# The keys' decay in a gated linear recurrence: a second, backward product scan in place of Ln and Exp

## The reference

```python
f = lb + (1.0 - lb) * sigmoid(f_logit)
k = 1.0 - f
q = silu(q_in) * HG_DK ** -0.5
S_t = diag(f_t) S_{t-1} + k_t^T v_t
o_t = S_t^T q_t
o = rms_norm(o) * silu(o_gate)
```

## Time and profile before

| | us |
|---|---|
| median of 3 runs (2399.16 to 2399.67) | 2399.17 |
| the profiled execution | 2399.41 |
| its span, slowest core (core 7) | 2397.9 |
| spans of all cores | 2392.3 to 2397.9 |

### The profile page before, as it was taken

The page is one execution under the profiler, slowest core; times in us unless marked ns, Lnnn a source line. Parts: engine busy times, 40 slices in busy tenths (PEclk is TensorE's granted clock), DMA queues, the critical chain, the costliest instruction groups (busy, mean ns, idle before and its releaser), DMA issues.

```text
span 2397.9 us, 40703 instructions; the slowest of 8 cores (2392.3 to 2397.9 us)
## 1 busy us (share of the span) xinstructions
PE 2323.3 (97%) x14144; PEld 1168.1 (49%) x14144; DVE 1311.1 (55%) x1977; ACT 1173.2 (49%) x1680; POOL 386.1 (16%) x515
## 2 busy tenths in 40 slices
PE   7999999999999889999999999999999999999998
PEld 3555555556555444444444444444444444444443
DVE  3666665666666874555553544536354545355334
ACT  4787788788888883444442331313222232224120
POOL 4444344344343340000000000000000000000000
PEclk9999999999999999999999999999999999999999
DMA  9566373564560555433335443434344333424240
GB/s 161 90 112 98 64 126 51 100 106 66 101 113 22 143 97 129 106 88 89 90 76 157 123 139 105 159 115 145 128 132 139 125 124 116 139 88 161 79 156 36
DMA packets 95977, 263.59 MB, mean 110 GB/s; under 512 B 9920, under 2 KB 34624, under 8 KB 92224
## 3 DMA queue, kind: packets, MB, share of 16 engines
q1 hardware_dynamic: 77008, 195.69, 25.1%
q0 software_dynamic: 18768, 65.28, 19.0%
HBM read 275.88 MB, written 61.87 MB: 141 GB/s over the span
## 4 chain that ended last, share of the span: by engine, by line
PE 87%; ACT 4%; DVE 4%; issue 3%; POOL 1%; DMA 1%; DVEq 0%; ACTq 0%; POOLq 0%; SPq 0%
PE psb L413 86%; ACT L434 1%; PE psb L418 1%; ACT sb_F L434 1%; DVE sb_YT L482 1%; DVE sb_Tb L466 1%; DVE sb_F L616 1%; DMA sb_W<-w 1%; ACT sb_U L434 0%; ACT sb_rso L434 0%; POOL sb_F L455 0%; DVE sb_ub L466 0%; DMA sb_y<-yD 0%; DVE sb_vt L473 0%; DVE sb_Qp L442 0%
## 5 line engine op out<-in xcount | busy, mean ns | idle before, releaser
L413 PE MATMUL psb<-sb_xT,sb_W 128*128 128x512 bf16 x2560 | 738.2, 383 | 28.2 <-DMA sb_xT<-xt 11.3
L413 PE MATMUL psb<-sb_hT,sb_f1r 128*128 128x512 bf16 x2816 | 681.2, 379 | 0.0
L434 ACT ACT_TABLE_LOAD x271 | 347.7, 1283 | 287.5 <-DVE sb_mv L908 129.7
L413 PEld LDWEIGHTS psb<-sb_hT,sb_f1r 128*128 128x128 bf16 x2816 | 273.4, 98 | 325.9
L413 PE MATMUL psb<-sb_W,sb_xT 128*128 128x128 bf16 x2048 | 402.6, 220 | 5.5 <-DVE sb_vt L473 4.1
L413 PE MATMUL psb<-sb_wf,sb_actb 128*128 128x512 bf16 x1408 | 346.4, 379 | 0.4 <-DVE sb_actb L442 0.3
L413 PEld LDWEIGHTS psb<-sb_xT,sb_W 128*128 128x128 bf16 x2560 | 239.7, 98 | 195.6 <-issue 45.0
L413 PE MATMUL psb<-sb_xT,sb_wj 128*128 128x512 bf16 x1024 | 314.9, 379 | 2.8 <-ACT sb_hT L434 1.3
L442 DVE TENSOR_TENSOR sb_actb<-sb_sg,psb 128x512 bf16<-128x512 f32 x176 | 118.6, 685 | 270.4 <-PE psb L413 168.0
L434 ACT ACTIVATE sb_sg<-psb 128x512 f32<-128x512 f32 x176 | 102.7, 596 | 296.2 <-PE psb L413 294.0
L413 PEld LDWEIGHTS psb<-sb_W,sb_xT 128*128 128x128 bf16 x2048 | 194.5, 98 | 69.4 <-issue 13.5
(11 more groups left out here) (91 smaller groups left out, 2760.3 us busy)
## 6 DMA issues: line engine op xcount, KB each, us to landing
...
```

Source lines behind the costliest of these rows:

```text
L413: return P.add("pe", lambda e: e.matmul(o, lhsT=l, rhs=r, start=start, stop=stop), ks(lhsT, rhs), out.k, dur=max(60, fsz(r)) / 2400.0 + 0. ...
L434: return P.add("act", lambda e: e.activation(out=o, in_=i, func=func, **kw), rd, out.k, dur=0.19 + fsz(o) / 1200.0 + 0.09 * ptr, tbl=ACT_S ...
```

## The change

The keys are no longer divided by D. A second scan, backwards along the frames, gives E, the product of the f from the frame after the key to the end of its half chunk. It reads f shifted by one (the new tile `fg` has one column more than the 512, which holds 1) and resets at the same mask. F3 x E is the key as it enters the state at the half chunk's end. This product is made on POOL now, straight into Kb. The first half's copy in the middle is scaled by e2 instead of e1, so Kb's last two pieces are what Kc was, and Kc and its product are gone; PE transposes Kb itself.

For the scores the query then has to be Qp divided by its half chunk's whole decay: a DVE reciprocal of the 8 end values of a tile into `Ei`, and a POOL product of Qp with it into `Qd`. The forward scan now writes over `fg`. Ln and Exp of D on ACT are gone. Counts per step: ACT loses 2 operations; DVE loses one product (Kb) and gets one scan and one reciprocal; POOL loses one product (Kc) and gets two (Kb, Qd).

```diff
--- before.py
+++ after.py
@@ -345,11 +345,13 @@
         Y2 = b("Y2", [32, 128], F32)
         YT = [b(f"YT{i}", [1024], F32) for i in range(4)]
         conv_end = b.at
-        F = [[b(f"F{i}_{p}", [TS], F32) for i in range(4)] for p in range(2)]
+        F = [[b(f"F{i}_{p}", [TS], F32) for i in range(3)] for p in range(2)]
+        fg = [b(f"fg{p}", [TS + 1], F32) for p in range(2)]
         Qp = [b(f"Qp{p}", [4, 128], BF16) for p in range(2)]
         Qx = [b(f"Qx{p}", [4, 64], BF16) for p in range(2)]
         Kb = [b(f"Kb{p}", [4, 192], BF16) for p in range(2)]
-        K2 = [b(f"Kc{p}", [4, 128], BF16) for p in range(2)]
+        Qd = [b(f"Qd{p}", [4, 128], BF16) for p in range(2)]
+        Ei = [b(f"Ei{p}", [8], F32) for p in range(2)]
         og = [b(f"og{p}", [TS], BF16) for p in range(2)]
         vt = [b(f"vt{p}", [4, 128], BF16) for p in range(2)]
         Kt = [b(f"Kt{p}", [4, 128], BF16) for p in range(2)]
@@ -555,6 +557,9 @@
         memset(scm.all(), 0.0)
         memset(V(scm.h[:, 0:TS:64], scm.all().k), 1.0)
         scanmask = scm.all()
+        endmask = scm.all()
+        for p in range(2):
+            memset(fg[p][TS:TS + 1], 1.0)
 
         one = sgl[0]
         memset(one[0:128], 1.0 / 128.0)
@@ -598,7 +603,7 @@
             if t == 0 and ("h", h) not in Wh:
                 Wh[("h", h)] = [wload(h, q) for q in range(4)]
             wq, wf, wo, wi = Wh[("h", h)]
-            F0, F1, F2, F3 = F[p]
+            F0, F1, F3 = F[p]
             for (w, dst, fn) in ((wf, F1, AF.Tanh), (wq, F0, AF.Silu), (wo, og[p], AF.Silu)):
                 ps = newps()
                 for kc in range(8):
@@ -609,13 +614,31 @@
                 relps(ps)
                 yield
                 if fn == AF.Tanh:
-                    ts(F2.all(), F1.all(), lbt[1, h:h + 1], lbt[3, h:h + 1], ALU.mult, ALU.add, eng="pool")
+                    f = fg[p]
+                    ts(f[0:TS], F1.all(), lbt[1, h:h + 1], lbt[3, h:h + 1], ALU.mult, ALU.add, eng="pool")
                     ts(F3.all(), F1.all(), lbt[2, h:h + 1], lbt[1, h:h + 1], ALU.mult, ALU.add, eng="pool")
 
-                    o, m, i2 = F1.all().ap, scanmask.ap, F2.all().ap
-                    P.add("dve", lambda e, o=o, m=m, i2=i2: e.tensor_tensor_scan(
-                        out=o, data0=m, data1=i2, initial=1.0, op0=ALU.max, op1=ALU.mult),
-                        ks(scanmask, F2.all()), F1.all().k, dur=1.3)
+
+                    fv = f.all()
+                    o, i1, m = F1.h[:, ::-1], f.h[:, TS:0:-1], endmask.ap
+                    P.add("dve", lambda e, o=o, m=m, i1=i1: e.tensor_tensor_scan(
+                        out=o, data0=i1, data1=m, initial=1.0, op0=ALU.mult, op1=ALU.max),
+                        ks(endmask, fv), F1.all().k, dur=1.3)
+                    o, m = f[0:TS].ap, scanmask.ap
+                    P.add("dve", lambda e, o=o, m=m: e.tensor_tensor_scan(
+                        out=o, data0=m, data1=o, initial=1.0, op0=ALU.max, op1=ALU.mult),
+                        ks(scanmask, f[0:TS]), f[0:TS].k, dur=1.3)
+                    kv = Kb[p]
+                    kout = V(kv.h[:].rearrange("p b (s q) -> p b s q", s=3)[:, :, 0:3:2, :], kv.all().k)
+                    tt(kout, V(F3.h[:].rearrange("p (b s q) -> p b s q", b=4, s=2), F3.all().k),
+                       V(F1.h[:].rearrange("p (b s q) -> p b s q", b=4, s=2), F1.all().k), ALU.mult, eng="pool")
+                    f2v = V(f.h[:, 0:TS].rearrange("p (b q) -> p b q", b=4), f[0:TS].k)
+                    e1 = V(f2v.ap[:, :, 63], f2v.k)
+                    e2 = V(f2v.ap[:, :, 127], f2v.k)
+                    tt(kv[:, 64:128], kv[:, 0:64], e2.bc(2, [128, 4, 64]), ALU.mult, eng="pool")
+                    o, i = Ei[p].all().ap, f.h[:, 63:TS:64]
+                    P.add("dve", lambda e, o=o, i=i: e.reciprocal(o, i), f2v.k, Ei[p].all().k, dur=0.25)
+                    tt(Eb[p].all(), e1, e2, ALU.mult, eng="pool")
             ps = newps()
             for tl in range(4):
                 for kc in range(8):
@@ -625,23 +648,12 @@
                     yield
             cp(vt[p].all(), pv3(ps, 4))
             relps(ps)
-            act(F2.all(), F1.all(), AF.Ln)
-            yield
-            f2v = V(F1.h[:].rearrange("p (b q) -> p b q", b=4), F1.all().k)
-            e1 = V(f2v.ap[:, :, 63], F1.all().k)
-            e2 = V(f2v.ap[:, :, 127], F1.all().k)
+            yield
+            q64 = Qp[p].all().r("p b (s q) -> p (b s) q", s=2)
             tt(Qp[p].all(), V(F0.h[:].rearrange("p (b q) -> p b q", b=4), F0.all().k), f2v, ALU.mult)
-            tt(Eb[p].all(), e1, e2, ALU.mult, eng="pool")
+            tt(Qd[p].all().r("p b (s q) -> p (b s) q", s=2), q64, Ei[p].all().bc(2, [128, 8, 64]), ALU.mult, eng="pool")
+            yield
             tt(Qx[p].all(), Qp[p][:, 64:128], e1.bc(2, [128, 4, 64]), ALU.mult)
-            act(F2.all(), F2.all(), AF.Exp, scale=-1.0)
-            yield
-            kv = Kb[p]
-            kout = V(kv.h[:].rearrange("p b (s q) -> p b s q", s=3)[:, :, 0:3:2, :], kv.all().k)
-            tt(kout, V(F3.h[:].rearrange("p (b s q) -> p b s q", b=4, s=2), F3.all().k),
-               V(F2.h[:].rearrange("p (b s q) -> p b s q", b=4, s=2), F2.all().k), ALU.mult)
-            yield
-            tt(kv[:, 64:128], kv[:, 0:64], e1.bc(2, [128, 4, 64]), ALU.mult, eng="pool")
-            tt(K2[p].all(), kv[:, 64:192], e2.bc(2, [128, 4, 128]), ALU.mult, eng="pool")
             yield
 
         def back(s):
@@ -650,7 +662,7 @@
             ps = newps()
             psv = V(psb[ps][:].bitcast(BF16), [("ps", ps)])
             for bb in range(4):
-                tr(V(psv.ap[:, bb * 128:bb * 128 + 128], psv.k), K2[p][bb, :])
+                tr(V(psv.ap[:, bb * 128:bb * 128 + 128], psv.k), Kb[p][bb, 64:192])
             cp(Kt[p].all(), V(psv.ap[:, 0:512].rearrange("p (a b) -> p a b", a=4), psv.k), eng="act")
             relps(ps)
             yield
@@ -658,7 +670,7 @@
             for bb in range(4):
                 for hf in range(2):
                     c0 = bb * 128 + hf * 64
-                    mm(pv(psA, c0, c0 + 64), Kb[p][bb, hf * 64:hf * 64 + 128], Qp[p][bb, hf * 64:hf * 64 + 64], True, True)
+                    mm(pv(psA, c0, c0 + 64), Kb[p][bb, hf * 64:hf * 64 + 128], Qd[p][bb, hf * 64:hf * 64 + 64], True, True)
             tt(Am[p].all(), pv3(psA, 4), mask.bc(1, [128, 4, 128]), ALU.mult)
             relps(psA)
             yield
```

## The result

The changed kernel took 2419.31 us (median of 6 runs, 2418.21 the lowest) against 2399.42 for the kernel before (6 runs): ratio 1.0079, 95% interval 1.0065 to 1.0093, so 19 us slower.

The account below looks back on a forecast made before the run. PE was taken to bound the kernel, 97% busy, with only its 42.5 us stage idle time and 28 us unseen waits recoverable. Terms -6, -5 (-9 and +4), -4 and +1 made -14 from 2399.4: 2385 us, range 2366 to 2405.

Parts of the forecast that it names:

- What goes: ACT loses each tile's Ln and Exp, 80 us, and 42 table loads, 54 us: 134 us in all.
- -6, -9 and -4: Gains in the stage, in us: PE's waits that ACT ends, waits DVE ends because it idles for ACT, unseen waits.
- The new instructions by themselves: Step pricing the added work: DVE 46 us more for second scan and reciprocal less a product, POOL 86 us more.
- The path: From forget gate's Tanh: keys 7.3 us now, 3.9 us to the transposes afterwards; scores 5.1 us; shorter if POOL and DVE are free.
- sum of -14: Total of all terms in us, including +1 for POOL's extra product in front of PE, giving 2385 us.
- The price of blocking: Rival, chance 0.05: DVE and POOL SBUF products block each other, 0.62 us in one tile of three, 13 us: 2398 us.
- My own test: Sign of a wrong forecast: POOL products whose mean is 0.3 us above 1.34.
- DVE's extra time: Term in the stage: DVE's extra 46 us take back a sixth of its idle time, +4 us.
- slower: Rival, chance 0.15: back-to-back scans on DVE delay sb_Am and state updates PE waits for, +28 less 14: 2413 us.
- The waits for ACT: PE's stage waits that ACT ends: 7.2 of 27.7 us, so 11 of the 42.5; half taken, -6 us.
- Tests that didn't fire: Signs of a wrong forecast: PE's waits for sb_Tb, sb_Am, sb_vt above 25 us together, or for sb_Qd above 5.
- Outside the stage: Sign: nothing changes from 1400 us on; a gain outside the stage would show the forecast wrong.

Follow-up runs that it names:

- e1: Kernel before without Ln and Exp of the forget product, keys multiplied by the decay instead of divided (computation changed): 2385.5 us, ratio 0.9943.
- e5: Control for e4: changed kernel with seven PSUM banks in the first stage, scans' mask in SBUF as before: 2453.5 us, ratio 1.0220.
- e4: Changed kernel with the scans' mask read from a PSUM bank, leaving seven banks for the first stage's matmuls: 2410.6 us (one run), no ratio.
- e10: Kernel before with a second scan into a scratch tile, result unused, both scans' mask in PSUM, seven banks: 2430.6 us, ratio 1.0124.
- e15: e11 with the key value F3 made on ACT instead of POOL and the key product on DVE: 2405.5 us, ratio 1.0015.
- e13: e11 with the key value F3 made on ACT in place of POOL: 2401.9 us, ratio 1.0000.
- e11: Changed kernel with the two scans in the other order, forward first, then backward: 2406.5 us, ratio 1.0022.

## Why the prediction was wrong

Forecast 2385 (2366 to 2405), measured 2419. The balance over the 40 tiles from the 8th to the 48th, where before to after is +17.8 us:

- ACT's relief, e1 less before: 530.9 - 541.0 = **-10**.
- The meetings, e5 less e4, on one and the same order: **+21**.
- The second scan in DVE's queue, e10 less before, less the bank: 553.8 - 541.0 - 6.3 = **+7**; if the bank cost nothing in e10, 13, and then the meetings are after less e4, 558.8 - 544.1 = 15.

Both ways the sum is +18, but the second is the first with the bank moved from one term to the other, and no second test. That it closes within half a microsecond is luck: effects of the order, which it has no term for, move such a stretch by up to 8 us. It also has no term for the key product that left DVE, nor for POOL's longer work, and that effects add up is an assumption. The split between the last two is known only to within 15 to 21 and 7 to 13; e15, 12 above e1, speaks for the upper end of the queue's share. Firm by itself is the +21, from two kernels in one order.

Point by point:

- **What goes, right.** 120 table loads in the stage were forecast and 120 counted; ACT was to be near 530 and is 541. My terms for it, -6, -9 and -4, made -19 before DVE's give-back, and e1 measured -14 (9 to 19). The way of pricing a relief by idle shares held within 5 us, at the edge of the interval.
- **The new instructions by themselves, right.** Backward scan 1.2 forecast, 1.21 undisturbed; reciprocal 0.2 and 0.197; key product 1.34 and 1.27; Qd 1.07 and 1.19.
- **The path, wrong, and the step that failed.** "Backward scan 1.2, product 1.3, forward scan beside it" put into one line two instructions that didn't run side by side with these operands. The line carried the condition "if POOL and DVE are free", and both were: they were not free of each other. The product took 2.2, so the keys come 0.9 us later than I had them, and the forward scan and Qp, when they are the later ones, shift the scores. So the sum of -14 had no term for meetings, where the runs showed +21 in 40 tiles.
- **The price of blocking, wrong.** I had the mechanism and its row, left it out of the sum, and priced it as a rival at one extra meeting of 0.62 us in a third of the tiles, 13 us, with a chance of 0.05. "Chance meetings" was the error: who releases whom stands in the diff. It is about one meeting a tile, of 0.9 us, and it cost 21 us in 40 tiles where I had 13 in all 64. My own test fired: the product's mean is 0.53 us above 1.34.
- **DVE's extra time, mis-sized.** +4 for 46 us of work all told. A second scan alone costs 7 to 13 us in 40 of 64 tiles (e10), and e15 has 12 over e1 with few of the scans' meetings left. A likely reason, not shown, is that PE's waits for DVE are not spread over DVE's idle time but sit behind the gate work. This was the rival "slower"; the runs support its mechanism, at a quarter to a half of its +28 in those 40 tiles.
- **The waits for ACT, undersized.** The 11 us of PE's 42.5 were scaled up from the six longest groups; over all groups it was 14.7, and in e1 5.3 are left.
- **Tests that didn't fire.** PE's waits for sb_Tb, sb_Am and sb_vt are 22.3 us together (limit 25) and for sb_Qd 4.3 (limit 5). The wait that grew most besides sb_Am, for the keys on POOL (9.3), wasn't on my list, though the change puts a POOL product straight in front of the transposes.
- **Outside the stage, right.** Nothing changed from 1400 us on. Just behind the stage PE now waits 5.1 us for the first DMAs of `sb_wj`, which POOL issues behind its longer queue. I had asked after that for the weights of the stage, not for these; but from the 64th tile to the end both kernels take 1513.3 us, so it costs nothing net.

Still open: why small edits of the order shift the time by up to 8 us either way; how the 12 us of e13 and e15 over e1 divide; how much of e13's gain over e11 (1.0000 against 1.0022, some 5 us) is POOL's load and how much fewer meetings; and the time of the key product in e11, below.
